# A bidirectional encoder layer with a mixture of experts: the router's logits with its weights held in the two halves of TensorE's array, three short moves beside them

## The reference

```
x = layer_norm(alpha * x + mix(x), ln1_g, ln1_b)
g_logits = t @ w_rg + b_rg                      # 4 groups
e_logits = t @ w_re + b_re                      # 32 experts
group: the largest of g_logits; in it the 2 largest of its 8 experts
weight = softmax(g_logits)[group] * (softmax over the group's experts, the two renormed)
for e in range(32):
    hg, hu = split(t @ w_gate_up[e])            # 1024 -> 2 x 256
    out += comb[:, e] * ((silu(hg) * hu) @ w_down[e])
x = layer_norm(alpha * x + out, ln2_g, ln2_b)
```

## Time and profile before

| | us |
|---|---|
| median of 3 runs | 485.21 (485.06 to 485.46) |
| profiled execution, its own time | 485.0 |
| its span, first to last instruction | 482.9 |
| PE busy | 464.1 (96%) |
| DVE busy | 242.2 (50%) |
| POOL busy | 222.9 (46%) |
| ACT busy | 207.2 (43%) |

### The profile page before, as it was taken

How to read it: one execution, slowest core, us unless ns; L and a number is a source line. 1 busy time by engine, 2 the same in 40 slices (tenths; PEclk the granted TensorE clock), 3 DMA queues, 4 the chain that set the end, 5 groups by cost and what they waited for, 6 DMA issues and landing times.

```text
span 482.9 us, 7627 instructions
## 1 busy us (share of the span) xinstructions
PE 464.1 (96%) x2776; PEld 326.1 (68%) x2776; DVE 242.2 (50%) x538; ACT 207.2 (43%) x457; POOL 222.9 (46%) x189
## 2 busy tenths in 40 slices
PE   8999999999999999989998999999999999999991
PEld 6999999988999999987883464444333444444431
DVE  2169999768997566381265442222222222222116
ACT  3544454578876679444566142121121222222212
POOL 2898989955966578979645221111001111111002
PEclk9999999999999999999989999999999999999997
DMA  8789988533533345555995999999999999999922
GB/s 292 257 335 369 366 294 347 183 126 129 176 132 132 130 132 173 178 174 175 421 422 217 392 425 395 421 423 421 421 420 421 421 421 421 423 420 421 422 84 88
DMA packets 26370, 145.12 MB, mean 300 GB/s; under 512 B 3040, under 2 KB 3296, under 8 KB 13792
## 3 DMA queue, kind: packets, MB, share of 16 engines
q1 hardware_dynamic: 26336, 144.65, 76.6%
HBM read 143.59 MB, written 1.05 MB: 300 GB/s over the span
## 4 chain that ended last, share of the span: by engine, by line
PE 90%; DVE 3%; ACT 3%; DMA 1%; issue 1%; POOL 1%; DVEq 0%; SPq 0%; ACTq 0%
PE bank L1539 23%; PE bank L1295 13%; PE bank L1297 12%; PE bank L1296 12%; PE bank L1574 12%; PE bank L1589 4%; PE bank L1590 3%; PE bank L1317 2%; PE bank L1373 1%; PE bank L1351 1%; DMA raw<-in_w_in 1%; PE bank L1563 1%; DVE stat L1051 1%; POOL w_lo L517 1%; PE bank L1380 1%
## 5 line engine op out<-in xcount | busy, mean ns | idle before, releaser
L517 POOL TENSOR_TENSOR w_lo<-raw,w_hi 128x512 fp32r<-128x512 f32 x140 | 182.9, 1323 | 50.5 <-ACT w_hi L585 46.9
L585 ACT CAST w_hi<-raw 128x512 fp32r<-128x512 f32 x140 | 85.2, 619 | 82.8 <-PE bank L1297 78.7
L1295 PE MATMUL bank<-x_hi,w_hi 128*128 128x256 f32 x400 | 115.5, 289 | 1.1 <-POOL w_lo L517 1.1
L1297 PE MATMUL bank<-x_hi,w_lo 128*128 128x256 f32 x400 | 113.3, 283 | 0.0
L1296 PE MATMUL bank<-x_lo,w_hi 128*128 128x256 f32 x400 | 113.3, 283 | 0.0
L850 DVE SCALAR_TENSOR_TENSOR bank<-slots,par,bank 128x256 f32<-128x256 f32 x232 | 92.3, 481 | 0.2
L546 POOL COPY raw<-gates 128x512 f32 x28 | 19.8, 706 | 152.8 <-PE bank L1539 134.5
L1539 PE MATMUL bank<-slots,raw 128*64 128x512 f32 x320 | 84.5, 593 | 0.0
L1295 PEld LDWEIGHTS bank<-x_hi,w_hi 128*128 128x128 f32 x400 | 76.8, 192 | 1.6 <-issue 1.3
L1296 PEld LDWEIGHTS bank<-x_lo,w_hi 128*128 128x128 f32 x400 | 76.8, 192 | 0.3
L1297 PEld LDWEIGHTS bank<-x_hi,w_lo 128*128 128x128 f32 x400 | 76.8, 192 | 0.0
(11 more groups left out here) (219 smaller groups left out, 651.9 us busy)
## 6 DMA issues: line engine op xcount, KB each, us to landing
slots<-in_w_gate_up SPq DMA_DIRECT2D x40, 1024.0 KB, 13.1
slots<-in_w_down SPq DMA_DIRECT2D x32, 1024.0 KB, 13.1
raw<-in_w_in SPq DMA_DIRECT2D x48, 512.0 KB, 3.8
extra<-in_w_gate_up SPq DMA_DIRECT2D x8, 1024.0 KB, 12.5
spare<-in_w_gate_up SPq DMA_DIRECT2D x8, 1024.0 KB, 15.9
late<-in_w_gate_up SPq DMA_DIRECT2D x8, 1024.0 KB, 15.1
raw<-in_w_attn SPq DMA_DIRECT2D x8, 512.0 KB, 3.2
raw<-in_w_conv SPq DMA_DIRECT2D x8, 512.0 KB, 3.5
```

What stands on the lines that cost most here:

```text
L517: nc.gpsimd.tensor_tensor(w_lo[:, n % SPLIT, m], raw[:, b % RAW, m], w_hi[:, n % SPLIT, m].bitcast(F32), ALU.subtract).then_inc(w_lo_done, 1)
L585: nc.scalar.copy(w_hi[:, n % SPLIT, m], raw[:, b % RAW, m]).then_inc(w_hi_done, 1)
L1295: mm(dst, ah, bh, start=first, stop=False, **kw)
L1297: return mm(dst, al, bh, start=False, stop=last, **kw)
```

## The change

The logits are made the other way round. `logit_parts` holds 64 columns of the router's weights (36 of the tile and what follows in memory, hence the padding of `wr_sb` by 32 columns, set to zero by POOL at the start) and streams 128 tokens. Even tiles k go to the lower half of the array and partitions 0 to 63 of the result, odd ones to the upper half. DVE copies each sum of 128 x 128 to SBUF (`parts`), and one product per token tile with `both_halves` (two shifted identities, added) adds the halves and turns the logits back to tokens in partitions. `WARM_ROUTE` falls from 5 to 3. On ACT the copy of the first turned piece goes ahead of the first deviation. On DVE the routing constants move from `B_OUT - 2` to `B_OUT + 2`, behind the last merge. PE makes pair 0's slot look-up in front of its products.

```diff
@@
 Q_BLOCK, V_BLOCK, GATE_BLOCK = 16, 28, 32
-WARM_START, WARM_ROUTE, WARM_PLACE = 3, 5, 1
+WARM_START, WARM_ROUTE, WARM_PLACE = 3, 3, 1
 RAW = 4
...
@@
         pT = sb("pT", [P, 2, TT, SEQ])
         sig_at = nc.sbuf_base
         sig = sb("sig", [P, 2, SEQ])
-        wr = sb("wr", [P, KT, LOGITS])
+        wr_sb = sb("wr", [P, KT * LOGITS + HALF_ROWS // 2])
+        wr = wr_sb[:, 0:KT * LOGITS].rearrange("p (k n) -> p k n", k=KT)
         x_at = nc.sbuf_base
         x_hi, x_lo = sb("x_hi", [P, KT, SEQ], F32R), sb("x_lo", [P, KT, SEQ], F32R)
         a_at = nc.sbuf_base
...
@@
         wr_sums = rt_flat[:, KT * LOGITS:(KT + 2) * LOGITS].rearrange("p (a n) -> p a n", a=2)
         masked = rt[:, 1:3, :, :].rearrange("p a t e -> p (a t e)")[:, 0:TT * (EXPERTS + NEEDLES)].rearrange(
             "p (t n) -> p t n", t=TT)
+        parts = [kT[:, 0, i * P:(i + 1) * P] for i in range(TT)]
+        both_halves = kT[:, 1, 64:64 + LOGITS]
         needles = rt[:, 3, 0, 0:TT * NEEDLES].rearrange("p (t n) -> p t n", t=TT)
         x1T = raw[:, 0:2, :].rearrange("p a (b t) -> p (a b) t", t=SEQ)
...
@@
         out_bank = [bank[3], bank[4], bank[5], bank[6]]
         first_choice = choice_sb[:]
         first_bank = [bank[1], bank[2], bank[3], bank[6]]
+        part_bank = [bank[7][:, 384:512], bank[1][:, 0:P]]
         logit_bank = bank[7][:, 0:TT * LOGITS].rearrange("p (t n) -> p t n", t=TT)
         lg = bank[7][:, P:P + TT * LOGITS].rearrange("p (t n) -> p t n", t=TT)
         group_key = rg[:, 2, :, :]
...
@@
         out_done, r_copied, z_done, x1_set = (sem(n) for n in ("out_done", "r_copied", "z_done", "x1_set"))
         r_turned, rT_by_act, rT_by_dve, logits_done = (
             sem(n) for n in ("r_turned", "rT_by_act", "rT_by_dve", "logits_done"))
+        parts_done, parts_copied = sem("parts_done"), sem("parts_copied")
         exp_in, router_exp, onehot_done, ranks_done, load_known = (
             sem(n) for n in ("exp_in", "router_exp", "onehot_done", "ranks_done", "load_known"))
         s_dist = sem("s_dist")
...
@@
             nc.gpsimd.memset(ones[:], 1.0)
             nc.gpsimd.memset(warm, 1.0).then_inc(warm_set, 1)
             nc.gpsimd.memset(h_pad, 0.0).then_inc(consts_set, 2)
+            nc.gpsimd.memset(wr_sb[:, KT * LOGITS:], 0.0)
             nc.gpsimd.memset(mean_ones[:], 1.0 / D).then_inc(consts_set, 1)
             nc.gpsimd.memset(eps[:], LN_EPS).then_inc(consts_set, 1)
...
@@
             nc.scalar.activation(sig[:, 0, 0:1], eps[:, 0:1], ACT.Sqrt)
             for n, (t, c) in enumerate(((0, 0), (1, 0), (0, 1), (1, 1))):
                 copy_r(n, t, c)
+            copy_rT(0, 0)
             deviation(0)
-            copy_rT(0, 0)
             deviation(1)
             copy_rT(2, 1)
             for t in range(TT):
...
...
-                if b == B_OUT - 2:
+                if b == B_OUT + 2:
                     nc.vector.memset(needles, NO_LOGIT)
                     nc.vector.memset(masked[:, :, EXPERTS:], NO_LOGIT)
                     for u in range(2):
                         for n in (0, 5):
                             nc.vector.tensor_copy(info[u][:, :, n:n + 1], con[:, C_TOKEN:C_TOKEN + TT].unsqueeze(2))
+                    nc.vector.tensor_tensor(both_halves, ident[:, 0:LOGITS], ident[:, HALF_ROWS:HALF_ROWS + LOGITS],
+                                            ALU.add)
                     nc.vector.tensor_copy(tri_r, tri)
                     nc.vector.tensor_copy(ones_r, ones[:]).then_inc(sums_ready, 1)
                     dve.wait_ge(sums_ready, 1)
...
@@
             inverse(0)
             shift(0, z_shift)
             copy_rT(3, 1)
+            for t in range(TT):
+                dve.wait_ge(parts_done, t + 1)
+                nc.vector.tensor_copy(parts[t], part_bank[t]).then_inc(parts_copied, 1)
             inverse(1)
             shift(1, z_shift)
...
@@
                     ins = nc.tensor.transpose(turned_bank[n][:, i * P:(i + 1) * P], xt[:, t, at * P:(at + 1) * P], ident)
                 ins.then_inc(r_turned, 1)
-            def logits(t, c):
+            def logit_parts(t, c):
                 for k in range(4 * c, 4 * c + 4):
-                    ins = mm(logit_bank[:, t, :], x1T[:, k, t * P:(t + 1) * P], wr[:, k, :],
-                             start=(t == 0 and k == 0), stop=(k == KT - 1), skip_group_check=True)
-                return ins
+                    rows_j = slice(k % 2 * HALF_ROWS, (k % 2 + 1) * HALF_ROWS)
+                    ins = mm(part_bank[t][rows_j, :], wr_sb[:, k * LOGITS:k * LOGITS + HALF_ROWS],
+                             x1T[:, k, t * P:(t + 1) * P], start=(k < 2), stop=(k >= KT - 2))
+                if c:
+                    ins.then_inc(parts_done, 1)
+
+            def logits(t):
+
+                pe.wait_ge(parts_copied, t + 1)
+                return mm(logit_bank[:, t, :], parts[t], both_halves, start=True, stop=True)
             turn_r(0, 0, 0)
             turn_r(1, 1, 0)
             turn_r(2, 0, 1)
             pe.wait_ge(rT_by_act, 1)
             turn_r(3, 1, 1)
-            logits(0, 0)
+            pe.wait_ge(wr_ready, 1)
+            pe.wait_ge(consts_set, 4)
+            logit_parts(0, 0)
             pe.wait_ge(rT_by_dve, 1)
-            logits(1, 0)
+            logit_parts(1, 0)
             pe.wait_ge(rT_by_act, 2)
-            logits(0, 1)
+            logit_parts(0, 1)
             pe.wait_ge(rT_by_dve, 2)
-            logits(1, 1).then_inc(logits_done, 1)
+            logit_parts(1, 1)
+            pe.wait_ge(sums_ready, 1)
+            logits(0)
+            logits(1).then_inc(logits_done, 1)
             keep_warm(bank[1][:, 0:SEQ], WARM_ROUTE)
-            pe.wait_ge(sums_ready, 1)
             pe.wait_ge(z_done, 2 * TT)
             pe.wait_ge(onehot_done, 1)
             mm(bank[4][:, 0:TT * EXPERTS], tri_r, onehot.rearrange("p t n -> p (t n)"), start=True, stop=False,
...
@@
                 down(p, (2 * u, 2 * u + 1))
             gather_first()
+            slot_info(0, 0)
             gate_up(0, 0)
-            slot_info(0, 0)
             for p in range(PAIRS):
                 pair(p)
             for c in range(2):
```

More of the change, by code:

```diff
@@ L35 @@
 LOGITS = GROUPS + EXPERTS
+HALF_ROWS = P // 2
 NEEDLES = 8
@@ L437, in _ @@
                     sp.dma_start(xt[:], x.rearrange("(t p) n -> p t n", p=P)).then_inc(s_xt, 16)
-                    sp.dma_start(wr[:], w_router).then_inc(s_wr, 16)
+                    sp.dma_start(wr, w_router).then_inc(s_wr, 16)
                 if b == 26:
@@ L1009, in _ @@
                                    for n in range(2)]
-                    chained(nc.vector.tensor_tensor(bias_wr, wr[:], per_channel[1], ALU.mult))
-                    chained(nc.vector.tensor_tensor(wr[:], wr[:], per_channel[0], ALU.mult))
-                    for a, w in enumerate((wr[:], bias_wr)):
+                    chained(nc.vector.tensor_tensor(bias_wr, wr, per_channel[1], ALU.mult))
+                    chained(nc.vector.tensor_tensor(wr, wr, per_channel[0], ALU.mult))
+                    for a, w in enumerate((wr, bias_wr)):
                         ins = nc.vector.tensor_reduce(wr_sums[:, a, :], w.rearrange("p k n -> p n k"), X_AXIS, ALU.add)
@@ L1017, in _ @@
                     dve.wait_ge(wr_means_done, 1)
-                    nc.vector.tensor_tensor(wr[:], wr[:], wr_bank[:, 0, :].unsqueeze(1).broadcast_to([P, KT, LOGITS]),
+                    nc.vector.tensor_tensor(wr, wr, wr_bank[:, 0, :].unsqueeze(1).broadcast_to([P, KT, LOGITS]),
                                             ALU.subtract)
```

## The result

The changed kernel takes 479.5 us (median of 4 runs, 478.6 to 480.18), the kernel before beside it 485.33 (485.06 to 486.04): ratio 0.9884, interval 0.9863 to 0.9905, so 5.6 us less (4.6 to 6.6). Two later comparisons gave 0.9888 (0.9868 to 0.9907) and 0.9895 (0.9876 to 0.9913). It is faster, as forecast, but 479.5 lies under the stated range (479.9 to 483.0). The profiled execution took 479.07, with a span of 477.3.

The account below looks back on a forecast made before the run. TensorE, carrying 90% of the chain, was taken as the bound. Terms of 1.9, 1.24, 0.45 and 0.72 us sum to 4.3, from 485.0 to 480.7, median 480.9; range 479.9 to 483.0.

Parts of the forecast that it names:

- Moved constants: Step into the output projection: routing constants behind VectorE's last merge end TensorE's waits, 1.9 us gained (1.45 to 2.1).
- Logits: Routing: half-width weight loads with both array halves streaming together bring the logits 1.24 us earlier; 0.35 us later without overlap.
- The rule on loads: Logit products: a weight load overlaps running products only in another row group; by it the logit term is near nothing.
- Warm products: Routing: three instead of five end before the choice, so the rank load follows it directly; 0.45 us gained (0.3 to 0.5).
- Slot look-up: First pair: look-up ahead of the products lets swish start at their end; 0.72 us gained (0.7 to 1.0).
- Sum at full clock: Whole kernel: the four terms add to 4.3 us, taken from the profiled 485.0, giving 480.7; 480.9 as median.
- Clock low in the gather: Rival: TensorE's clock halves during part of the gather, costing 1.0 us, 481.9; chance 0.3 (whole gather 483.8, 0.08).
- The halves don't overlap: Rival: at 128 columns the array halves run in series, logit term -0.35 instead of 1.24 us, 482.5; chance 0.1.
- moving the constants doesn't free PE: Rival at the output projection: the residual is late for another reason, the 1.9 us are not gained, 482.8; chance 0.07.

Follow-up runs that it names:

- act_back: Changed kernel with ScalarE's first deviation back in front of its first copy of turned rows; 0.9894 of the kernel before, stretch to the logits 5.39 us against 4.97.
- before_act: Kernel before with only ScalarE's first copy of turned rows moved ahead of its first deviation; ratio 0.9985, stretch to the logits 5.59 us against 6.18.
- one_half: Changed kernel with all eight tiles of a token tile held one after the other in the array's lower half, join over 64 rows; 0.9934 of before, 481.76 us.
- before_again: Kernel before, unedited, profiled once more; its routing took 1.4 us more and its start 1.8 us less than in the profile used for the prediction.
- before_slot: Kernel before with only the first pair's slot look-up moved in front of its products; 0.9977 of the kernel before.
- const_alone: Kernel before with only the routing constants moved behind the last merge on VectorE; 0.9957 of the kernel before.

## Why the prediction missed

The sign held, and so did the mechanisms of three of the four terms; the time fell 0.4 us below the range and 1.4 below the forecast. Step by step:

- **Moved constants, "1.9 us (1.45 to 2.1)".** 2.35 us. The chain was as described, the sizes were not. I read the waits from idle times: 1.45 us ahead of the first product and 0.43 us of a weight load, and bounded all that lies behind the first at 0.65. The start times of PE's products say 1.61 us at the first and 0.75 behind it, spread over two blocks.
- **Logits, "1.24 us".** 1.21, and the steps came as forecast. The last group's loads begin at 240.13, 0.06 us behind DVE's second copy (239.39 + 0.68), so that copy was the gate; the prediction had 0.05. What I overlooked is what ACT's exchange gave by the prediction's own numbers: without it three groups of 0.48 us from 242.25 end at 243.69, behind the copy, and the last group is 0.47 us later. act_back (0.42) and before_act (0.59) measure that. The expectation of act_back, "nothing lost", was the error, not the term.
- **The rule on loads.** The rule in the Trainium skill, page "TensorE: Matmul & The Clock Gate", section "The mechanism", by which a load overlaps running products only in another row group, doesn't hold here as it stands: 24 loads of 64 columns took 1.33 us while records of the same row groups streamed. In one_half even loads into the same half were hidden: 32 records of 128 columns start 0.11 us apart, which is what streaming alone takes (a quarter of 0.43 us for 512 columns).
- **Warm products, "0.45 us".** This mechanism failed. The stretch from the logits to the ranks fell by 0.52, but not by the count: at full clock five cost nothing, in the changed kernel (3.54) and in before_act (3.53). The low clock over them was the cost, and behind the new logit products the clock fell ahead of the rank products in none of eleven profiles, behind the old ones in six of seven.
- **Slot look-up, "0.72 us".** 0.9: the look-up in front costs 0.12 us, as it does where PE runs on, and I had charged the 0.33 that it took where PE's pipeline drained.
- **"Sum at full clock ... Against the profiled execution's own 485.0".** This step failed most. Between the two profiles the terms measure 2.36 + 1.21 + 0.53 + 0.89 = 5.0 us (spans: 482.9 - 477.3 = 5.6; the other 0.6 is the quicker start in the profile after, 0.74, less 0.1 at the end). But the 0.53 is the clock. With both kernels at full clock the terms give 2.36 + 1.21 + 0 + 0.89 = 4.46 us. That this lies so near the 4.3 of the forecast is luck: 0.45 too little for the constants and 0.17 for the look-up stand against 0.45 too much for the warm products. The three comparisons gave 5.6, 5.4 and 5.1 us, which is 0.6 to 1.2 above 4.46 (the interval of the last, 4.2 to 6.0, still takes it in). That rest is what I had at nothing.
- **The clock, taken as a loss only.** I treated the clock only as a loss that might come with the change, and the profile before as what the kernel before always does. Against 6.18 us to the logits and 3.53 on to the ranks at full clock, that profile lost 0.5 us, before_again 1.95, before_slot and const_alone 1.8, and three of six profiles with the look-up behind lost 1.3 to 2.5 us after the first pair. Of the changed kernel's three profiles one lost 1.16 us in the gather, and none lost anything in the logits, the ranks or behind the first pair. That the rest comes from this difference is the reading that fits all profiles; its exact share can't be had from one profile a run.
- **The rivals.** "Clock low in the gather" (480.9 + 1.0) occurs, with 1.2 to 1.4 us, in four of the seven profiles with the new logits and three warm products; the time is still lower than forecast, since the kernel before loses as much or more. "The halves don't overlap" and "moving the constants doesn't free PE" are excluded. No wait of PE for an expert's weights shows in the profile after; the last stretch stayed at 220.0.

## What to carry to other kernels

Before work is put into an engine's queue for its idle time, look at who waits for the instruction behind it: 4 us of constants on an engine half idle cost 2.35 us of TensorE, three engines further on. Where a product's streaming operand is shorter than its load, hold the narrow operand in both halves of the array and stream the wide one; the halves really run together. And profile a kernel of this kind two or three times before predicting from it: compare untouched stretches first, and look in each for stretches at a granted clock of 0.50. A loss that comes in some executions only is part of the time before, and a change that removes it gains more than its terms at full clock.

## What the runs showed of the hardware

TensorE's granted clock fell at different places in executions of the same program: the kernel before lost it from 245.8 to 249.3 us in one profile and from 243.7 to 250.5 in another. The first 32 records took 7.17 us in fifteen profiles and 8.98 to 9.10 in three, on the same instructions, started within 0.35 us of each other. In the slow ones the records start 0.43 us apart up to 10.3 to 10.7 us and 0.22 apart from there on, which is the ratio of the two clock levels, 1.2 and 2.4 GHz, although the windows of the profile print 1.00 there. Logit products at 36 columns in 0.11 us slots, whose records kept the engine busy all the time, were followed by 0.50 in six of seven profiles and by 1.00 in before_act. At the hand-overs of the first pair 3.0 us with 1.02 us of busy time (262 to 265 in before_again) kept 1.00, while in const_alone the clock fell at 261.8 after 0.77 us of busy time in the two from 259. These rows give no rule for it.

Casts on DVE were slow while POOL was subtracting: 1.2 to 1.4 us for 128 x 2 elements, against 0.23 us for 128 x 4 at 248.98 in the profile after. One and the same cast of 128 x 128 (`ones_r`) shows it best. In the kernel before it took 0.21 us at 212.86, just after POOL had run dry at 212.85; in the changed kernel, behind the merges, it took 1.33 us at 223.91, in the middle of POOL's subtractions. No run tested the cause alone. So the block of constants costs DVE 4 us because of where it stands; behind the last merge it runs until 225.2 and nobody waits for it, since DVE's next work begins at 235.57.
